# A fp32 decoder layer on one core: memory keys and values placed ahead of the state outputs, and four edits beside it

## The reference, cut to what matters

```
xn = rmsnorm(x) ; proj = xn @ w_in              # gate 512 | x_rg 512 | u_s5 512
# recurrence (512 channels, 4 blocks of 128)
r, i = sigmoid(xc @ rg_wa + ba), sigmoid(xc @ rg_wx + bx)      # xc: causal conv of x_rg
log_a = -8 r softplus(-lambda) ; a = exp(log_a) ; mult = sqrt(-expm1(2 log_a)), 1 at token 0
h_t = a_t h_(t-1) + mult * i * xc ; y_rg = h * gelu(gate)
# S5: 32 groups of 16 channels, 64 complex states each
h_t = abar h_(t-1) + bbar u_t ; y = Re(C h) + d u ; z = gelu(y) ; y_s5 = z * sigmoid(z @ glu_w + b)
x = x + [y_rg | y_s5] @ w_out
# attention, 4 heads, into 256 memory tokens
k, v = rmsnorm(mem) @ xa_wkv ; q = rmsnorm(x) @ xa_wq
x = x + softmax(q k / 16) v @ xa_wo
# then the experts: top 4 of 32, clamped SwiGLU; and a final norm
```

## Time and profile before

| | us |
|---|---|
| median of 3 runs | 2511.12 (2510.06 to 2511.14) |
| the profiled execution | 2509.66 |
| its span, first to last instruction | 2507.9 |
| PE busy | 2348.3 (94%) |
| DVE busy | 1545.0 (62%) |
| ACT busy | 1122.4 (45%) |
| POOL busy | 389.7 (16%) |

### The profile page before, as it was taken

The page is one execution under the profiler, slowest core; times in us unless marked ns, Lnnn a source line. Parts: engine busy times, 40 slices in busy tenths (PEclk is TensorE's granted clock), DMA queues, the critical chain, the costliest instruction groups (busy, mean ns, idle before and its releaser), DMA issues.

```text
span 2507.9 us, 31481 instructions
## 1 busy us (share of the span) xinstructions
PE 2348.3 (94%) x9546; PEld 1719.6 (69%) x9547; DVE 1545.0 (62%) x1505; ACT 1122.4 (45%) x1051; POOL 389.7 (16%) x344
## 2 busy tenths in 40 slices
PE   7998299998989968999999999999999999999995
PEld 4563274464464546888888888888888888888883
DVE  4537851101052257786777766677779887997783
ACT  4123102013032134564654544556567666774663
POOL 0361400000000001121211211211112112211211
PEclk9989659997999988999999999999999999999997
DMA  5001001040001137886986866879789979997894
GB/s 157 34 1 53 33 9 76 34 150 18 34 34 61 59 126 274 297 313 215 308 301 225 282 210 228 286 234 307 275 303 363 364 270 316 381 383 272 306 330 159
DMA packets 212944, 506.63 MB, mean 202 GB/s; under 512 B 19172, under 2 KB 19400, under 8 KB 211688
## 3 DMA queue, kind: packets, MB, share of 16 engines
q1 hardware_dynamic: 196912, 459.98, 50.7%
q0 software_dynamic: 14032, 45.77, 7.2%
q10 hardware_dynamic: 1960, 0.35, 0.1%
HBM read 469.62 MB, written 35.26 MB: 201 GB/s over the span
## 4 chain that ended last, share of the span: by engine, by line
PE 82%; DVE 9%; issue 4%; ACT 3%; DMA 1%; ACTq 0%; DVEq 0%; SPq 0%; POOLq 0%
PE PS L575 27%; PE PS L880 21%; PE PS L901 12%; PE PS L884 10%; PE PS L908 6%; DVE WL L1671 2%; PE PS L933 1%; PE PS L872 1%; PE PS L838 1%; DVE H L1443 1%; ACT WA L971 1%; ACT YT L971 1%; DVE WA L1273 1%; DVE WA L1479 1%; PE PS L963 1%
## 5 line engine op out<-in xcount | busy, mean ns | idle before, releaser
L1671 DVE TENSOR_TENSOR WL<-WA,WH 128x2048 fp32r<-128x2048 f32 x256 | 582.2, 2287 | 179.8 <-ACT WH L1193 114.6
L880 PE MATMUL PS<-WH,XEH 128*128 128x512 f32 x1344 | 361.5, 391 | 0.2 <-DVE WL L1671 0.2
L880 PE MATMUL PS<-WH,XEL 128*128 128x512 f32 x1344 | 361.2, 391 | 0.0
L1671 DVE TENSOR_TENSOR WL<-H,WH 128x2048 fp32r<-128x2048 f32 x128 | 292.9, 2289 | 92.1 <-ACT WH L1172 64.5
L884 PE MATMUL PS<-WL,XEH 128*128 128x512 f32 x1344 | 346.8, 390 | 0.0
L1193 ACT CAST WH<-WA 128x2048 fp32r<-128x2048 f32 x124 | 236.7, 1910 | 205.2 <-PE PS L908 203.2
L880 PEld LDWEIGHTS PS<-WH,XEL 128*128 128x128 f32 x1344 | 253.4, 189 | 53.4
L880 PEld LDWEIGHTS PS<-WH,XEH 128*128 128x128 f32 x1344 | 253.4, 189 | 52.7 <-DVE WL L1671 0.6
L884 PEld LDWEIGHTS PS<-WL,XEH 128*128 128x128 f32 x1344 | 252.9, 188 | 52.8
L575 PE MATMUL PS<-WB,YT 128*128 128x512 f32 x512 | 224.6, 597 | 2.6 <-DVE YT L1273 1.6
L575 PE MATMUL PS<-XT,WB 128*128 128x512 f32 x512 | 223.1, 597 | 1.1 <-issue 1.1
(11 more groups left out here) (280 smaller groups left out, 2721.3 us busy)
## 6 DMA issues: line engine op xcount, KB each, us to landing
WA<-in_exp_w_gu SPq DMA_DIRECT2D x192, 1024.0 KB, 8.3
H<-in_exp_w_gu SPq DMA_DIRECT2D x64, 1024.0 KB
WA<-in_exp_w_down SPq DMA_DIRECT2D x64, 1024.0 KB, 7.0
H<-in_exp_w_down SPq DMA_DIRECT2D x64, 1024.0 KB, 8.7
WB<-in_xa_wkv SPq DMA_DIRECT2D x4, 2048.0 KB, 7.8
WB<-in_w_in SPq DMA_DIRECT2D x3, 2048.0 KB, 11.0
y_acc<-H SPq DMA_DIRECT2D x9, 512.0 KB, 2.6
H<-in_x SPq DMA_DIRECT2D x4, 1024.0 KB, 5.8
```

Source lines behind the costliest of these rows:

```text
L880: nc.tensor.matmul(PS[:, 2 * h + t, :], x[:, KT4 * half + k, t * P:(t + 1) * P], WH[:, j % 4, k * HALF:(k + 1) * HALF], start=False, stop= ...
L1671: v.tensor_tensor(WL[:, s, :], src, WH[:, s, :].bitcast(F32), sub).then_inc(done, 1)
```

## The change

- *Memory ahead.* The units `mt`, `kk` and `vv` stand between the state products `s` and the outputs `y`. The kv chunks are loaded ahead of o1, mem is loaded when `g` is done, and the keys and values are written into the upper half of `H` (`KTN`, `VVN`), from which a DMA on SP's queue moves them to `WA` behind the loads of x. DVE waits for that DMA (`kv_moved`) before it writes tile 4 of `H`.
- *State products copied.* ACT copies `s` from PSUM to `SR`; DVE reads them there.
- *Decay by exponential.* ACT makes a = exp(8 log-scale (r)) itself, with one activation beside the tanh; the reciprocal and two more passes of DVE go, and the tanh and root that gave the multiplier are used in another form. The next block's `conv` moves ahead of this block's scan. In PE's order the gate products of the last block stand behind `ut`.
- *Filter tables.* POOL builds the rotation table `RT` after `rgc_done` in place of `kts_done`, and `FM` right behind it, in the place of `GM` once that has been transposed; `MM` and its DMAs come last. The load of s5_d goes behind the first norm.
- *Block-diagonal taps.* DVE lays C out in two diagonal blocks (`CCB`), so that 32 products of 128 rows by 32 columns make the taps.
- *Norms.* The first norm's scaling goes from ACT to DVE. In the second norm nothing is scaled: `xt2` transposes `H` itself, tile by tile between the last `wo1` units, and 1/rms of a token enters the scale of the softmax (`RS`, `NRS`).

```diff
-        for ct in range(CT):
-            if ct + 1 < CT:
-                order += rg("xr", ct + 1)
-            order += zz(ct)
-            if ct + 1 < CT:
-                order += rg("g", ct + 1)
-        order += [("ut", n) for n in range(8)]
+        for ct in range(CT - 1):
+            order += rg("xr", ct + 1) + zz(ct) + rg("g", ct + 1)
+        order += [("ut", n) for n in range(8)] + zz(CT - 1)
         for n in range(4):
             order += [("s", 0, n), ("s", 1, n)]
+        order += [("mt", m, h) for m in range(MT) for h in range(2)]
+        order += [("kk", j) for j in range(K)] + [("vv", c, m) for c in range(2) for m in range(MT)]
         order += [("y", n) for n in range(8)]
...
-        order += [("wo1", c, l) for c in range(2) for l in range(L)]
...
+        order += [("wo1", 0, l) for l in range(L)]
+        for l in range(L + 1):
+            order += [("wo1", 1, l)] * (l < L)
+            order += [("xt2", l - 1, h) for h in range(2) if l > 0]
...
+                    units_read(sp, "kk")
+                    units_read(sp, "vv")
+                    sp.dma_start(KV, Hf[:, 4096:8192]).then_inc(kv_moved, 16)
...
-                 GM[r, w2, q, :, :].rearrange("p a b -> p (a b)"), CC[r, w2, q, :], w2, 2)
+                 GM[:, w2, q, :, :].rearrange("p a b -> p (a b)"),
+                 CCB[:, w2, q, :, :].rearrange("p a b -> p (a b)"), w2, 2)
...
-                act.wait_ge(rstd_done[n], l + 1)
-                a(dst, src, ACT.Copy, scale=sm[:, c0 + 16:c0 + 17], s=xn_done[n])
...
+            def rg_decay(ct):
+                if ct == 2:
+                    act.wait_ge(mm_in, 16 * L)
+                neg = V[:, V_LAM + ct:V_LAM + ct + 1]
+                a(YT[:, ct, :], TH, ACT.Exp, bias=neg, scale=neg)
+                a(TH, TH, ACT.Tanh, bias=sm[:, 100 + ct:101 + ct], scale=sm[:, 100 + ct:101 + ct])
                 a(TH, TH, ACT.Sqrt, s=rg_sq)
...
+            act.wait_ge(mem_in, 16)
+            for m in range(MT):
+                root(1, MEM[:, m, :], MEMT.rearrange("p k s -> p (k s)")[:, m * D:(m + 1) * D], 104 + m)
+            rg_gates(CT - 1)
+            for n in range(4):
+                wait_filled(act, ("s", 1, n))
+                for w in range(2):
+                    copy_unit(("s", w, n), SR[:, w, 4 * n:4 * n + 4, :].rearrange("p q k -> p (q k)"))
+            rg_decay(CT - 1)
+            act.wait_ge(rg_done, CT)
...
-                                               bias=sm[:, 24 + 2 * b + hh:25 + 2 * b + hh], scale=HD ** -0.5,
+                                               bias=sm[:, 24 + 2 * b + hh:25 + 2 * b + hh], scale=RS[:, l:l + 1],
...
+            for l in range(L + 1):
+                if l < L:
+                    rstd(0, l, l)
+                    ts(YT[:, l, :], H[:, l, :], sm[:, l + 16:l + 17], None, mul, s=xn_done[0])
...
-                dve.wait_ge(rg_tp, ct + 1)
-                ts(QQ, TH, 1.0, None, add, s=rg_q)
-                d(v.reciprocal(QQ, QQ))
                 stt(TI, TI, 1.0, XC, add, mul)
-                ts(XC, QQ, 2.0, -1.0, mul, add)
+                if ct + 1 < CT:
+                    wait_filled(dve, ("z", ct, 0, 1))
+                    conv(ct + 1)
+                else:
+                    for m in range(MT):
+                        for h in range(2):
+                            scaled(("mt", m, h), MEMT[:, 4 * h:4 * h + 4, m * P:(m + 1) * P], V_MEM + 4 * h)
                 dve.wait_ge(rg_sq, ct + 1)
-                tt(QQ, QQ, TH, mul)
-                d(v.memset(QQ[:, 0:1], 0.5))
+                stt(QQ, YT[:, ct, :], 1.0, TH, add, mul)
+                d(v.memset(QQ[:, 0:1], 1.0))
                 tt(TI, TI, QQ, mul)
-                d(v.tensor_tensor_scan(QQ, XC, TI, 0.0, mul, add))
+                d(v.tensor_tensor_scan(QQ, YT[:, ct, :], TI, 0.0, mul, add))
...
-            pool.wait_ge(kts_done, 1)
+            pool.wait_ge(rgc_done, 1)
```

More of the change, by code:

```diff
@@ L592, in tile_transposes @@
                     end((kind, l, h), ins)
-            def transposes(kind, norm, src):
-                for l in range(L):
-                    tile_transposes(kind, l, norm, src)
-            transposes("xt", 0, YT)
-            pe.wait_ge(par_in, 16 * 7)
+            for l in range(L):
+                tile_transposes("xt", l, YT)
+            pe.wait_ge(par_in, 16 * 6)
             for w, u in enumerate((("cre",), ("cim",))):
@@ L649, in _ @@
             pe.wait_ge(blk_in, 16 * 12)
-            for ct in range(CT):
-                if ct + 1 < CT:
-                    proj("xr", ct + 1)
+            for ct in range(CT - 1):
+                proj("xr", ct + 1)
                 gates(ct)
-                if ct + 1 < CT:
-                    proj("g", ct + 1)
+                proj("g", ct + 1)
             units_read(pe, "u")
@@ L664, in _ @@
                 end(("ut", n), ins)
+            gates(CT - 1)
             units_read(pe, "em")
@@ L675, in _ @@
                     end(("s", w2, n), ins)
+            for m in range(MT):
+                pe.wait_ge(xn_done[1], m + 1)
+                for h in range(2):
+                    o = begin(("mt", m, h))
+                    for k in range(4):
+                        c = (4 * h + k) * P
+                        ins = nc.tensor.transpose(o[:, k * P:(k + 1) * P], MEM[:, m, c:c + P], ident[:])
+                    end(("mt", m, h), ins)
+            units_read(pe, "mt")
+            for c in range(2):
+                w = weights(("kv", c))
+                for j in range(4):
+                    o = begin(("kk", 4 * c + j))
+                    for k in range(K):
+                        ins = mm(o[:, 0:ML], w[:, k, j * P:(j + 1) * P], MEMT[:, k, :], k, K)
+                    end(("kk", 4 * c + j), ins)
+            for c in range(2):
+                w = weights(("kv", 2 + c))
+                for m in range(MT):
+                    o = begin(("vv", c, m))
+                    for k in range(K):
+                        ins = mm(o, MEMT[:, k, m * P:(m + 1) * P], w[:, k, :], k, K)
+                    end(("vv", c, m), ins)
             pe.wait_ge(mm_in, 16 * L)
@@ L998, in _ @@
                     act.wait_ge(x_in[l // 2], 16)
-                norm(0, l, H[:, l, :], YT[:, l, :], l)
+                root(0, H[:, l, :], YT[:, l, :], l)
             act.wait_ge(zeroed, 3)
@@ L1314, in _ @@
                      u, own=True)
-            dve.wait_ge(xn_done[0], L)
+                for b in range(2):
+                    r = slice(NS * b, NS * b + NS)
+                    d(v.tensor_copy(CCB[r, w, :, b, :], CC[r, w, :, :]))
             d(v.memset(XRg[:, 0:4], 0.0), xr_zero)
@@ L1432, in _ @@
             dve.wait_ge(db_done, 1)
-            for b in range(2):
-                u = ("ktap", b)
-                wait_filled(dve, u)
-                evac(dve, v.tensor_tensor(KTS.rearrange("p (q b c) -> p b q c", q=Q, b=2)[:, b],
-                                          bank(u)[:, 0:Q * SC].rearrange("p (q c) -> p q c", q=Q),
-                                          DB.rearrange("p (q b c) -> p b q c", q=Q, b=2)[:, b], add), u, own=True)
+            wait_filled(dve, ("ktap",))
+            evac(dve, v.tensor_tensor(KTS, bank(("ktap",)), DB, add), ("ktap",), own=True)
@@ L1492, in _ @@
                 tt(y, y, SG[:, n % 2, :], mul, s=glu_done)
[L1493 removed]
+            dve.wait_ge(x_again, 16)
             for c in range(2):
[L1495 to L1507 removed]
+                for l in range(L + 1):
+                    if l < L:
+                        u = ("wo1", c, l)
+                        cc = slice(c * HALF, (c + 1) * HALF)
+                        if c == 0 and l == L // 2:
+                            dve.wait_ge(kv_moved, 16)
+                        wait_filled(dve, u)
+                        evac(dve, v.tensor_tensor(H[:, l, cc], bank(u), XR0[:, l, cc], add), u, own=True)
+                        dve.sem_inc(h1_done, 1)
+                    if c == 1 and l > 0:
+                        for h in range(2):
+                            scaled(("xt2", l - 1, h), XT[:, 4 * h:4 * h + 4, (l - 1) * P:l * P], V_XA + 4 * h)
+            for l in range(L):
+                rstd(2, l, l)
+            ts(RS, sm[:, 16:24], HD ** -0.5, None, mul)
+            ts(NRS, RS, -1.0, None, mul)
             def maxima(n):
@@ L1893, in _ @@
                 tt(FM[:, 1, qs], TF1, TF2, sub, s=f_done)
+            d(g.memset(MM, 0.0))
+            pool.wait_ge(kts_done, 1)
+            for l in range(L):
+                pool.dma_start(MM[0:(l + 1) * SC, l, :], KTS[(L - 1 - l) * SC:P, :]).then_inc(mm_in, 16)
             pool.wait_ge(h2_done, 1)
```

234 lines of the change are left out of this document (91 added, 143 removed).

## The result

| | before | after |
|---|---|---|
| median, us | 2510.59 (2509.86 to 2511.14) | 2383.89 (2379.96 to 2385.30, 4 runs) |
| ratio | | 0.9493, 95% interval 0.9477 to 0.9509 |
| the profiled execution | 2509.66 | 2385.03 |
| PE busy | 2348.3 (94%) | 2285.1 (96%) |

The kernel is 5% faster, 127 us in the medians and 124.6 in the profiled executions. The forecast was 2412 with a range from 2385 to 2434: the direction was right, and the time lies 28 us under the forecast and 1 us under the lower end. One step makes up most of it. The table by stage shows which, in the same form as before: length, PE busy, PEld, DVE, ACT, POOL, then the clock, DMA share and GB/s.

A forecast was written before the change was run, and what follows sets the result against it. PE's chain was taken as the bound (82% PE, 9% DVE). Terms 4.8 + 13.9 + 20.0 + 37.0 + 3.0 + 18.2 + 2.3 = 99.2 off 2509.66 gave 2410.5, 2412 on the medians' scale; range 2385 to 2434.

The forecast's parts named there:

- the state outputs: The 96 products of `y`: a few us at fast clock, then slow at 0.50, 3 us gained (0 to 26).
- The rival with this mechanism: State outputs `y` run fast because PE comes hot: 33 to 38 us instead of 57, total about 2390; chance 0.2.
- First norm: Start of the kernel: scaling moved from ACT to DVE, projection at 31.0 instead of 35.8, 4.8 us gained.
- Taps: Taps and their transposes: 64 records instead of 128, stage 30.5 to 16.6 us, 13.9 us gained (11.5 to 19).
- Recurrence: Recurrence stage up to `ut`: PE runs through without waiting for the convolution, 20.0 us gained (14 to 21).
- State stage and memory: From `ut` to `y`, with keys and values: the 30 us `HP` wait vanishes, 37.0 us gained (25 to 39).
- The new chain on ACT: Behind `ut`: ACT's squares, roots, tanh and copies of `s` in a row, keys starting about 241.5, 18.7 us.
- `zt` and `glu`: The stage behind the state outputs: keeps its 17.1 us.
- `wo1` and the second norm: Output projection keeps 110.0 us; the norm's 27.3 us stage becomes 9.1 of threaded transposes and waits, 18.2 us gained.
- The copy of keys and values: Rival at `wo1`: DVE waits for this copy before tile 4; matters only if over 35 us; chance 0.02.
- the bound given for this part: The part behind the scores: the prediction is wrong if it changes by more than 3 us.
- The rule that spoke against it: Skill page: clock follows how busy PE is, so `y` would run at 1.00; the prediction followed the trace's 0.50 instead.

The follow-up runs named there:

- the run with both edits back: The changed kernel with DVE's reciprocal and passes in place of ACT's exponential, and the next block's convolution behind the gate multiplication again: 2390.83 us.
- its two variants: The kernel before with thirty unread dense products in its pause for `HP`, 2507.55 us; the kernel before with the block-diagonal taps alone, 2497.87 us.
- the first experiment: The changed kernel with PE waiting for all of `HP` before the first state output, a pause of 5 us: 2416.7 us.
- the fifth experiment: The kernel before with thirty dense products that nobody reads in PE's 30 us pause for `HP`: 2507.55 us, ratio 0.9994.

## Why the prediction was right, and where it was not

**The step that failed: the state outputs.** The prediction said of them "I take it that they cannot hold it: a few us fast, then slow", 3 us gained with 57 left. They held the clock and took 33.8, so the term was 26.2. The fault is in the argument: two observations were joined that don't belong together. The taps lost the clock in gapless work, but their products have 16 columns, those of `y` 128. (That the columns make the difference isn't isolated: transposes of 128 columns raised the clock, which the products of `y` never did.) And that `y` had not raised the clock in 60 us doesn't show that it could not hold it: the runs with a pause show `y` staying at 0.50, those without, or with dense products behind the pause, show it staying at 1.00. The rival with this mechanism had a chance of 0.2 and came true; its 33 to 38 us for `y` hold the measured 33.8, and its time, about 2390, was closer. The range's lower end, 2385, was set too high beside it, since the fast outputs and the better ends of the other terms can come together.

**The others, by their own steps.**
- First norm, 4.8 forecast with ends of 4.0 and 5.5, 6.4 measured. ACT had been the pace and DVE became it, as said. Its cycle is 2.18 per tile, not 2.3. PE's eight transposes took 1.09 us with pauses of 1.09, where the run with ACT's scaling has 1.97 with pauses of 0.98: a difference of clock that isn't explained by the pauses, and that costs nothing, since in the run with both edits back the cycle was 2.18 with either. Two other runs (the convolution behind the scan, the taps mixed) show PE waiting 0.97 and 0.96 us for the weights, until 29.22 and 29.08: the DMA is now the next limit, and it came over 2 us before the 31.6 that the prediction reads from the kernel before.
- Taps, 13.9 forecast, 15.0 measured, with the shape foreseen: 64 records, at 1.00 first, at 0.50 in between. Only the moment of the fall varies, and with it the time of the same 64 records, 8.05 to 11.03 us. That the forecast of 10.5 came within 0.3 of the 10.78 is partly luck.
- Recurrence, 20.0 forecast. 92.7 us without a wait, and 3.5 for the last gate products behind `ut`: 96.2, as summed. The price of a record in that sum is right, but not its words: the 82.5 us are 96 products, or 192 records, of 0.43 each. The reason given is right only in part. The prediction took the gain from the exponential and the early convolution; the run without both loses 8.9 us of the 20.0, and the rest came from POOL's tables ending sooner and from the last gates standing behind `ut`.
- State stage and memory, 37.0 forecast. From `ut` to `y` are 73.9 us, less 3.5 for the gate products 70.4 against 70.8. The new chain on ACT, called the least sure step, cost PE one wait of 0.75, and DVE's gains one of 1.65; the load of mem did not show. The keys ran at full clock from their start (27.86 us for 128 records), as the prediction took it from the earlier trace rows. Moving the memory back costs 52 us, of which its 26.8 of waiting belong to this term.
- `zt` and `glu`: 15.0 where 17.1 was kept, because they too begin at 1.00.
- `wo1` and the second norm, 119.1 us forecast and measured (342.96 to 462.02); `q` 110.1, both.
- The copy of keys and values ran 17.5 us from issue to landing and nobody waited.
- Behind `q` 2.9 us more than before, inside the bound given for this part. From kernel to kernel this part takes 1808.3 to 1812.4 us among the changed ones and 1808.3 to 1808.7 in the kernel before and its two variants. No run isolates it.

From the forecast's 2410.5 this gives: 2.8 less at `y`'s start, 23.2 in `y`, 2.1 in `zt` and `glu`, and 2.9 more behind `q`: 2385.3, where 2385.03 was profiled.

**The rule that spoke against it.** The Trainium skill ("TensorE: Matmul & The Clock Gate", Part 1) has the clock follow PE's activity. The prediction held the row of the slow `y` against it, and the outcome by the Trainium skill was right here: with PE kept busy, `y` ran at 1.00. Yet that rule alone doesn't give what followed the pauses: PE 15.00 of 15.00 us busy and the clock at 0.50 (the first experiment, 330 to 345). What the runs show is that idle time, or the taps in a row, can take the clock away, that dense products or transposes bring it back, and that the products of `y` leave it where it is. What sets `y` apart from them isn't isolated.

## What to carry to other kernels

Ask of a slow stage not only how long it is, but at what clock PE comes to it: a pause of 2.5 to 5 us in front of or in `y` cost up to 26 us of clock here. Real work moved into the pause avoids that, and so do a few dense products behind it, at their own price (8.6 us here). Work moved into a wait is worth the wait and the clock of what follows; a filler without use (the fifth experiment) is worth nothing where another engine is still the pace. A run of very small products that loses the clock is better spread among dense ones (5 us here).

## What the runs showed of the hardware

- The state outputs, 96 products or 192 records, run without a gap at either clock for their whole length: 33.8 us at 1.00, 60.0 at 0.50, a factor of 1.78.
- The clock was at 1.00 before pauses of 4.97 and 2.53 us and at 0.50 behind them. The changed kernel's pauses of 0.75 to 1.74 us from `ut` to `q` left it at 1.00, but one of 0.96 behind `y` took it in the run with the pause filled. Dense products of 512 columns brought it back (0.50 to 0.51 from 300 to 303, 1.00 from 303 on, in the run with the warm-up).
- The tap records, 128 rows by 32 columns, lost the clock when they ran in a row without any idle time, and kept it between products of 512 columns. The changed kernel's taps:

```profile
112.10:114.00 1.90, 1.90 (x19) 1.88 (x17) 0.00 (x0) 1.10 (x1) 1.82 (x2) 1.00 0.00 0
114.00:116.00 2.00, 2.00 (x17) 2.00 (x16) 0.00 (x0) 0.00 (x0) 1.84 (x3) 0.83 0.00 0
116.00:118.00 2.00, 2.00 (x11) 2.00 (x11) 0.00 (x0) 0.00 (x0) 1.59 (x6) 0.50 0.00 0
```

- In the first norm of the kernel before, the PEclk column says 1.00, but eight transposes take 1.97 us, as long as at 0.50 in the run with both edits back (23 to 26 us), where they take 1.09 at 1.00. So at the start of a trace the length of the records is the better witness of the clock.
- DVE's passes slow down beside POOL's table work, though not all: the same three convolution passes took 8.99 us in the first block, where POOL was busy for 24.08 of the 25 us from 140 to 165, and 3.92 in the second, where it was for 3.80 of 17. The reciprocal took 6.55 us with POOL busy and without. In the changed kernel DVE had the slack and no PE wait came of it; in the kernel before it was 6 us of waiting.

```profile
149.21 8.99 DVE L1282 SCALAR_TENSOR_TENSOR H<-H,V 128x1024 f32<-128x1024 f32 x3
...
177.13 3.92 DVE L1282 SCALAR_TENSOR_TENSOR H<-H,V 128x1024 f32<-128x1024 f32 x3
```
